# Norm with output projection on one Trainium2 core: layer norm as two VectorE operations, the cast on ScalarE, and the first tile's products given part by part

## The reference, cut to what matters

```
y     = mix @ w_out[layer]                                  # [tokens, 1024] @ [1024, 1024]
h_mid = layer_norm(ALPHA * h + gate * y, ln_g, ln_b)        # over the 1024 values of a token
u     = layer_norm_plain(h_mid) * (1 + scale) + shift       # the operand of the feed-forward part
```

## Time and profile before

| | us |
|---|---|
| median of 3 runs (lowest, highest) | 4234.38 (4233.95, 4239.08) |
| the profiled execution | 4238.0 |
| its span | 4236.2 |
| PE busy | 3569.1 (84%) |
| POOL busy | 1765.3 (42%) |
| DVE busy | 1616.5 (38%) |
| ACT busy | 1474.8 (35%) |

### The profile page before, as it was taken

How to read it: one execution, slowest core, us unless ns; L and a number is a source line. 1 busy time by engine, 2 the same in 40 slices (tenths; PEclk the granted TensorE clock), 3 DMA queues, 4 the chain that set the end, 5 groups by cost and what they waited for, 6 DMA issues and landing times. The chain is left out here.

```text
span 4236.2 us, 54980 instructions
## 1 busy us (share of the span) xinstructions
PE 3569.1 (84%) x21518; PEld 2940.0 (69%) x21518; DVE 1616.5 (38%) x2584; ACT 1474.8 (35%) x2437; POOL 1765.3 (42%) x1150
## 2 busy tenths in 40 slices
PE   6799596877686999998898599596867869998897
PEld 2488486565475888887787487485644758887786
DVE  2104553755473221224333205555745622223224
ACT  2211274765443111113332311475834422222222
POOL 1211242763344334445555211344822445555554
PEclk8899698888897999999999799697989989999998
DMA  8423312113332112222332223213064333232332
GB/s 293 148 85 116 102 26 65 30 32 84 103 100 95 60 60 70 65 65 81 108 97 92 88 87 111 89 28 75 12 199 134 105 100 95 90 98 92 100 100 90
DMA packets 170474, 388.51 MB, mean 92 GB/s; under 512 B 14312, under 2 KB 74824, under 8 KB 170256
## 3 DMA queue, kind: packets, MB, share of 16 engines
q1 hardware_dynamic: 147808, 330.96, 25.3%
q10 hardware_dynamic: 19200, 44.63, 2.8%
q0 software_dynamic: 3248, 9.90, 0.9%
HBM read 319.41 MB, written 66.03 MB: 91 GB/s over the span
## 5 line engine op out<-in xcount | busy, mean ns | idle before, releaser
L2279 POOL TENSOR_TENSOR ffn_wlo<-ffn_raw,ffn_whi 128x1024 fp32r<-128x1024 f32 x264 | 639.4, 2430 | 727.9 <-ACT ffn_whi L2204 727.8
L2204 ACT CAST ffn_whi<-ffn_raw 128x1024 fp32r<-128x1024 f32 x264 | 272.3, 1049 | 841.3 <-PE ffn_acc L127 434.1
L125 PE MATMUL ffn_gate<-second_uhi,ffn_whi 128*128 128x256 f32 (+1 forms) x1144 | 376.8, 329 | 53.2 <-POOL ffn_wlo L2279 36.9
L2418 DVE TENSOR_TENSOR ffn_silu<-ffn_up,ffn_silu 128x256 f32<-128x256 f32 (+1 forms) x143 | 74.8, 526 | 879.6 <-PE ffn_up L127 863.6
L125 PE MATMUL ffn_acc<-ffn_whi,ffn_hhi 128*128 128x512 f32 x792 | 321.0, 405 | 65.0 <-issue 43.9
L126 PE MATMUL ffn_gate<-second_ulo,ffn_whi 128*128 128x256 f32 (+1 forms) x1144 | 375.6, 328 | 0.0
L127 PE MATMUL ffn_gate<-second_uhi,ffn_wlo 128*128 128x256 f32 (+1 forms) x1144 | 375.4, 328 | 0.0
L126 PE MATMUL ffn_up<-second_ulo,ffn_whi 128*128 128x256 f32 (+1 forms) x1144 | 370.6, 324 | 0.0
L125 PE MATMUL ffn_up<-second_uhi,ffn_whi 128*128 128x256 f32 (+1 forms) x1144 | 370.6, 324 | 0.0
L127 PE MATMUL ffn_up<-second_uhi,ffn_wlo 128*128 128x256 f32 (+1 forms) x1144 | 370.3, 324 | 0.0
L2430 DVE TENSOR_TENSOR y<-ffn_acc,y 128x512 f32<-128x512 f32 x360 | 248.4, 691 | 289.8 <-PE ffn_acc L127 289.8
(11 more groups left out here) (283 smaller groups left out, 8177.6 us busy)
## 6 DMA issues: line engine op xcount, KB each, us to landing
ffn_raw<-w_ffn_dram SPq DMA_DIRECT2D x264, 512.0 KB, 3.6
in_raw<-w_in_dram SPq DMA_DIRECT2D x42, 512.0 KB, 3.6
norm_input_ada_w<-w_ada_dram SPq DMA_DIRECT2D x10, 2048.0 KB, 8.2
swa_ada_w<-w_ada_dram SPq DMA_DIRECT2D x8, 2048.0 KB
proj_scratch<-in_stage ACTq DMA_DIRECT2D x20, 640.0 KB, 2.9
ada_w<-w_ada_dram SPq DMA_DIRECT2D x6, 2048.0 KB
gla_kq<-proj_scratch SPq DMA_DIRECT2D x32, 320.0 KB
swa_qhl<-heads_scratch SPq DMA_DIRECT2D x36, 256.0 KB
```

The source lines that it names most:

```text
L125: pe.matmul(out, st_hi, mv_hi, start=start, stop=False)
L2204: act.copy(whi[:, w % 3, :], raw[:, w % 2, :]).then_inc(w_hi, 1)
L2279: pool.tensor_tensor(wlo[:, w % 3, :], raw[:, w % 2, :], whi[:, w % 3, :].bitcast(F32), ALU.subtract).then_inc(w_ready, 1)
L2418: dve.tensor_tensor(sg[:, n % 2, 0:tn], UP[:, n % 2, 0:tn], sg[:, n % 2, 0:tn], ALU.mult).then_inc(mul_done, 1)
```

## The change

In `norm_tiles` with kind "attention":

- **The first norm** is two VectorE operations in place of one ScalarE, one GpSimd and one VectorE operation: h = (h - mean) * ln_g, then h = h * rstd + ln_b. `nmu` of the first norm is gone.
- **Order on DVE**: the second statistics of a tile follow its first norm at once, in the step of `SUM`. The second `normalizers` (reciprocal and nmu) open the next step.
- **Order on ACT**: the second norm of tile r-2 (x = ...) opens the step, ahead of tile r's `mhi`. Both square roots of a tile are in the step of `SUM`.
- **The cast** to `uhi` is on ACT in place of DVE, between the two square roots.
- **The start**: the first tile's `mix` is loaded ahead of the weights and its `mhi` cast ahead of theirs. TensorE takes the first tile's products part by part (k outermost), waiting for `wo_lo` of each part. GpSimd no longer waits for the constants before its first `mlo`.

The diff, cut to its core:

```diff
         @block.sync
         def _(sp):
+            def mixed_columns(sp, i, s):
+                sp.dma_start(mix[:, 0, :, :], t["mix"].rearrange("(k p) n -> p k n", p=P)[:, :, bass.ds(i * 2 * P + s * P, P)]).then_inc(mix_in, 16)
+
             if attn:
+                mixed_columns(sp, first_pair, 0)
                 for k in range(KT):
...
-                    if attn:
+                    if attn and not first_tile(i, r):
                         wait_count(sp, mix_lo, count(i, r) - 1)
...
         @block.tensor
         def _(pe):
-            if attn:
-                pe.wait_ge(wo_lo, KT)
-
             def step(i, r, live):
                 if attn and live(0):
                     s = r % 2
                     pe.wait_ge(mix_lo, count(i, r))
                     wait_count(pe, gated, count(i, r) - 2)
-                    for half in range(2):
-                        for k in range(KT):
-                            cols = slice(half * BANK, (half + 1) * BANK)
...
+                    first = first_tile(i, r)
+                    order = [(k, half) for k in range(KT) for half in range(2)] if first else [(k, half) for half in range(2) for k in range(KT)]
+                    for k, half in order:
+                        if first:
+                            pe.wait_ge(wo_lo, k + 1)
+                        cols = slice(half * BANK, (half + 1) * BANK)
...
             def step(i, r, live):
+                if post and live(NEXT):
+                    normalizers(i, r - NEXT, 1)
                 if post and live(SUM):
...
                     statistics(i, u, 0, h)
-                if post and live(NEXT):
-                    u, s = r - NEXT, (r - NEXT) % 2
-                    dve.wait_ge(h_scaled, count(i, u))
-                    dve.tensor_tensor(h[:, s, :], h[:, s, :], lnb[:, :], ALU.add).then_inc(h_done, 1)
-                if post and live(SUM):
-                    normalizers(i, r - SUM, 0)
...
+                    dve.wait_ge(mv_done[0], count(i, u))
+                    dve.scalar_tensor_tensor(h[:, s, :], h[:, s, :], mv[:, s, 0, 0:1], lng[:, :], ALU.subtract, ALU.mult).then_inc(centered, 1)
+                    inverse(i, u, 0)
+                    dve.wait_ge(centered, count(i, u))
+                    dve.scalar_tensor_tensor(h[:, s, :], h[:, s, :], rstd[:, s, 0:1], lnb[:, :], ALU.mult, ALU.add).then_inc(h_done, 1)
+                    dve.wait_ge(h_done, count(i, u))
+                    statistics(i, u, 1, h)
...
             act.wait_ge(eps_set, 1)
             if attn:
+                act.wait_ge(mix_in, 16)
+                act.copy(mhi[:, 0, :, :], mix[:, 0, :, :]).then_inc(mix_hi, 1)
                 for k in range(KT):
...
             def step(i, r, live):
-                if attn and live(0):
+                if post and live(NEXT):
+                    normalize(i, r - NEXT)
+                if attn and live(0) and not first_tile(i, r):
...
                 if post and live(SUM):
-                    normalize(i, r - SUM, 0, h)
-                if modulated and live(NEXT):
-                    normalize(i, r - NEXT, 1, x)
+                    deviation(i, r - SUM, 0)
+                if post and live(SPLIT):
+                    u, s = r - SPLIT, (r - SPLIT) % 2
+                    act.wait_ge(u_done, count(i, u))
+                    act.copy(uhi[:, :, bass.ds(i * 2 * P + u * P, P)], x[:, s, :].rearrange("p (k n) -> p k n", k=KT)).then_inc(u_hi, 1)
+                if post and live(SUM):
+                    deviation(i, r - SUM, 1)
...
-            pool.wait_ge(const_in, const_loads)
+            if not post:
+                pool.wait_ge(const_in, const_loads)
...
-                if post and live(SUM):
-                    u, s = r - SUM, (r - SUM) % 2
-                    pool.wait_ge(normed[0], count(i, u))
-                    pool.tensor_tensor(h[:, s, :], h[:, s, :], lng[:, :], ALU.mult).then_inc(h_scaled, 1)
```

More of the change, by code:

```diff
@@ L351, in step @@
                     s = r % 2
-                    if attn:
+                    if attn and not first_tile(i, r):
                         wait_count(sp, mix_lo, count(i, r) - 1)
-                        sp.dma_start(mix[:, 0, :, :], t["mix"].rearrange("(k p) n -> p k n", p=P)[:, :, bass.ds(i * 2 * P + s * P, P)]).then_inc(mix_in, 16)
+                        mixed_columns(sp, i, s)
                     wait_count(sp, summed if post else normed[1], count(i, r) - 2)
@@ L385, in step @@
                     wait_count(pe, gated, count(i, r) - 2)
-                    for half in range(2):
-                        for k in range(KT):
-                            cols = slice(half * BANK, (half + 1) * BANK)
-                            mm = product(pe, Y[:, s, cols], mhi[:, s, k, :], mlo[:, s, k, :],
-                                         wohi[:, k, cols], wolo[:, k, cols], k == 0, k == KT - 1)
+                    first = first_tile(i, r)
[4 more added lines that the diff above has]
+                        cols = slice(half * BANK, (half + 1) * BANK)
+                        mm = product(pe, Y[:, s, cols], mhi[:, s, k, :], mlo[:, s, k, :],
+                                             wohi[:, k, cols], wolo[:, k, cols], k == 0, k == KT - 1)
                     mm.then_inc(y_done, 1)
@@ L433, in normalizers @@
                 dve.wait_ge(rs_done[j], count(i, u))
+            def normalizers(i, u, j):
+                s = u % 2
+                inverse(i, u, j)
                 dve.scalar_tensor_tensor(nmu[:, s, j:j + 1], mv[:, s, j, 0:1], -1.0, rstd[:, s, j:j + 1], ALU.mult, ALU.mult).then_inc(nm_done[j], 1)
             def step(i, r, live):
+                if post and live(NEXT):
+                    normalizers(i, r - NEXT, 1)
                 if post and live(SUM):
@@ L469, in step @@
                     dve.tensor_copy(uhi[:, :, bass.ds(i * 2 * P + u * P, P)], x[:, s, :].rearrange("p (k n) -> p k n", k=KT)).then_inc(u_hi, 1)
-                if modulated and live(NEXT):
+                if not post and live(NEXT):
                     normalizers(i, r - NEXT, 1)
@@ L495, in normalize @@
                 act.activation(sd[:, s, j:j + 1], mv[:, s, j, 1:2], ACT.Sqrt, bias=eps[:, 0:1]).then_inc(sd_done[j], 1)
-                act.wait_ge(nm_done[j], count(i, u))
-                if j == 1:
-                    wait_count(act, u_lo, count(i, u) - 2)
-                act.activation(dst[:, s, :], h[:, s, :], ACT.Identity, scale=rstd[:, s, j:j + 1], bias=nmu[:, s, j:j + 1]).then_inc(normed[j], 1)
+            def normalize(i, u):
+                s = u % 2
+                act.wait_ge(nm_done[1], count(i, u))
+                wait_count(act, u_lo, count(i, u) - 2)
+                act.activation(x[:, s, :], h[:, s, :], ACT.Identity, scale=rstd[:, s, 1:2], bias=nmu[:, s, 1:2]).then_inc(normed[1], 1)
             def step(i, r, live):
-                if attn and live(0):
+                if post and live(NEXT):
+                    normalize(i, r - NEXT)
+                if attn and live(0) and not first_tile(i, r):
                     s = r % 2
@@ L506, in step @@
                     act.copy(mhi[:, s, :, :], mix[:, 0, :, :]).then_inc(mix_hi, 1)
-                if modulated and live(SPLIT):
+                if live(SPLIT):
                     u, s = r - SPLIT, (r - SPLIT) % 2
@@ L514, in step @@
                 if post and live(SUM):
-                    normalize(i, r - SUM, 0, h)
-                if modulated and live(NEXT):
-                    normalize(i, r - NEXT, 1, x)
+                    deviation(i, r - SUM, 0)
[5 more added lines that the diff above has]
+                    deviation(i, r - SUM, 1)
+                if not post and live(NEXT):
+                    deviation(i, r - NEXT, 1)
+                    normalize(i, r - NEXT)
             stagger(act, step)
```

16 lines of the change are left out of this document (8 added, 8 removed).

## The result

The changed kernel took 4203.3 us (median of 4 runs, 4198.7 to 4205.5) beside 4236.7 for the kernel before on the same chip: ratio 0.992, interval 0.9902 to 0.9937. That is 33.4 us less; 58.6 less was forecast. The profiled run took 4198.7, its span is 4196.9.

What follows compares the result with a forecast made beforehand. PE, busy 84% and mostly in feed-forward, was taken to bound the kernel; the change acts only in two norm stages. Layer 0's 32.7 and layer 1's 25.9 made 58.6 us: 4234.4 - 58.6 = 4176, range 4164 to 4202.

Steps and rivals of the forecast that it cites:

- the lead of 0.13 us: h * rstd + ln_b starts 0.13 us before `ulo`, counting t from the start of a tile's L447.
- GpSimd goes first: Rival, 17%: `ulo` starts before h * rstd + ln_b, which ends 2.3 late; the ring is 13.7 to 14.8, total 4200.
- Opening: Start of each layer's stage: early `mix` and products part by part bring the third tile 8.8 us earlier.
- t(0): Start of the first tile's L447 in layer 0, forecast at 1157.2, 11.9 us earlier.
- t(2): Start of the third tile's L447, where the loop begins, forecast 8.8 us earlier in each layer.
- the upper case: Opening, second tile: from `mlo`'s end to L447 11.3 to 12.9 us, the upper figure with slow clock.
- Loop: Tiles between opening and drain: 12.6 us each, gaining 13.7 us in layer 0 and 6.9 in layer 1.
- the ring: Path from a tile's L447 through norm, `mhi`, `mlo` and products to L447 two tiles on: 25.2 us, 12.6 per tile.
- Slow clock: Loop: PE waits 0.8 us per tile with the clock near 1.00, so no loss was priced.
- Drain: From each layer's last L447 to the end of the last `ulo`: 20.8 us instead of 30.98, gain 10.2.
- New operations take 2.45: Rival, 3%: both new norm operations take 2.45 us each; the ring is 13.8, gain 24.4 us less, total 4200.
- Cover of the cast on ACT: Loop: cast ends by t + 5.6, second sd wanted at t + 8.4, 2.8 us cover; without it 0.5 per tile.

Runs made afterwards that it cites:

- `ulo` behind the norm: The change plus a GpSimd wait for DVE's second norm operation before `ulo`; 4183.9 us, ratio 0.9867.
- nudge: The change plus three 128x1 copies on ACT ahead of its cast to `uhi`, no wait added; 4183.4 us, ratio 0.987.
- filler: The change with `ulo` waiting for DVE's second norm operation, plus four overwritten 128x512 matmuls per tile before PE's wait for `mlo`; 4181.5 us, ratio 0.9867.

## Why the prediction was wrong, point by point

- **The step that failed** is the lead of 0.13 us between h * rstd + ln_b at t + 5.47 and `ulo` at t + 5.6. The sum took the operation at its unhindered 1.23 in every tile; it took 3.2 to 3.5 in 13 of the 14 tiles in which it meets an `ulo`. I took the sd's 0.29 as its cost to ACT and let the cast start 0.31 after it; it starts 0.20 after it. And I took L466 to cost 1.28 to the next start; with the reciprocal between, L469 stands 1.40 behind. Together 0.23, which turns a lead of 0.13 into a lag of 0.1 (measured in the tile above: 0.09; over the 13 tiles from a lag of 0.23 to a lead of 0.05). A true lead of 0.13 would have been enough: 0.06 was. The rival *GpSimd goes first* (17%) is what happened, at its upper end: 14.9 and 14.4 per tile, since `mlo` did also run into L462. It gave 4200, the measurement is 4203. A lead of 0.13, less than the rows were good for as the prediction itself said, deserved near even chances and not 17%. How much hung on it: with the order mended and nothing else changed, the kernel is 55.5 (`ulo` behind the norm) and 56.6 (nudge) less than before, against the 58.6 of the sum.
- *Opening*: right. t(0) 12.2 earlier after the stage's start (11.9 forecast), t(2) 8.3 and 9.6 (8.8 each); 9 to 10 per layer when undone elsewhere. The last `wolo` ended 2.8 later, not 2.1, but t(0) followed 1.9 behind it, not 2.9: two misses that cancelled, so t(0) came out closer than its terms. Tile 1's wait of 2.39 and slow clock (0.74) were forecast as the upper case.
- *Loop*: -13.7 and -6.9 forecast, +2.1 and +2.2 measured. In the tile read, 2.11 of the ring's excess is L469 behind `ulo` and 1.27 L462 beside `mlo` (0.3 to 1.9 in the six tiles after it). With the order mended the ring is 25.7 or less (filler), against the 25.2 of the sum.
- *Slow clock*: I priced none, for waits of 0.8. They came in lumps: the ring spans two tiles, so the wait gathers in every second one, and 1.9 at once was followed by 0.66 of the clock, while the earlier trace rows's tiles of layer 1 kept 1.00. A wait of a given length did not settle it: in layer 0 of the change the clock kept 1.00 behind 2.56 and 2.81 and fell to 0.66 behind 2.01, 2.63 and 2.72. This is the second, smaller omission. Its size stays open: between the profiled loops of *`ulo` behind the norm* and *filler* lie 7 x 0.4 + 5 x 1.2, about 9 us of waits and slow clock together, between their medians only 2.4.
- *Drain*: -8.2 in place of -10.2 per layer; the last tile's L469 also fell behind `ulo` (3.32). With the order mended it is 20.9, against 20.8 forecast.
- *New operations take 2.45*: no. They took 1.28 in every tile where GpSimd was out of the way, so no run here shows what the Trainium skill's rule says ("Vector Engine (DVE) Microarchitecture Reference", "Points that are easy to get wrong"), half the throughput for two such sources; the measurement decides, for this operation on 128x1024 of 32-bit data.
- *Cover of the cast on ACT*: right that the second sd was not held (it started 0.24 behind its aggregate in the change); wrong to see in the cast's place only ACT's own time. Its start also sets when GpSimd starts.

Sum: 58.6 forecast; less 15.8 and 9.1 in the loops and 2.0 in each drain, plus 0.3 in the openings, is 30.0, the two stages as measured.

## What to carry to other kernels

Where a two-input operation of VectorE and one of GpSimd become ready within a few tenths of each other, write both orders down and give each its price and a near even chance, or settle the order in the code. Here 0.1 us decided over about 20 us, and the cheapest cure was a wait on the engine that is off the path. When an operation is moved, ask for every buffer and every queue behind it (x behind `ulo`, `mix` behind the store of h): in two of these runs the gain was lost on waits that no price of the operation itself shows.
